# One joint norm between two transformer blocks, squares added up on GpSimd, output stored in pieces, weight splits and first loads in another order

## What is computed

```
h  = rms_norm(x, gain) * (1 + scale) + shift      # ahead of every mixer and every feed-forward net
x  = x + gate * y                                  # after each of them
x1 = rms_norm(x, final_norm_g)                     # end of the first block: the x of the second
h  = rms_norm(x1, norm1_g_2) * (1 + scale) + shift # first thing the second block does
```

## Time and profile before

| | us |
|---|---|
| median of three executions | 3278.46 |
| profiled execution, its own time | 3276.97 |
| span of its trace | 3275.2 |
| TensorE busy | 3024.4 (92%) |
| VectorE busy | 1440.7 (44%) |
| ScalarE busy | 1134.9 (35%) |
| GpSimd busy | 194.5 (6%) |

### The profile page before, as it was taken

One profiled execution on the slowest core, in us unless ns is written; L12 is line 12 of the kernel. 1 busy time (PEld: TensorE's weight loads), 2 busy tenths in 40 slices (PEclk: granted clock), 3 DMA queues, 4 the chain that ended last, 5 costly groups with the idle time before them and its releaser, 6 DMA issues.

```text
span 3275.2 us, 34399 instructions
## 1 busy us (share of the span) xinstructions
PE 3024.4 (92%) x14360; PEld 2379.1 (73%) x14360; DVE 1440.7 (44%) x1884; ACT 1134.9 (35%) x1396; POOL 194.5 (6%) x199
## 2 busy tenths in 40 slices
PE   5998888899999888999998999989899999999998
PEld 3875666678877777857776887777676667778876
DVE  5474444354433554534456434245443344433322
ACT  3364222232222444334543222134433345432221
POOL 0011222000000010001000000000100010000000
PEclk8998787899999999999999999999999999999999
DMA  7430000133433211413223343331131121222221
GB/s 263 174 132 19 1 1 1 60 146 135 155 109 122 79 51 52 171 45 119 71 84 135 142 154 138 119 116 52 46 139 58 67 71 46 96 79 101 91 92 49
DMA packets 46278, 309.68 MB, mean 95 GB/s; under 512 B 5339, under 2 KB 6235, under 8 KB 12844
## 3 DMA queue, kind: packets, MB, share of 16 engines
q1 hardware_dynamic: 43964, 297.32, 25.2%
q0 software_dynamic: 2160, 10.16, 0.9%
HBM read 302.74 MB, written 4.72 MB: 94 GB/s over the span
## 4 chain that ended last, share of the span: by engine, by line
PE 57%; ACT 6%; DVE 3%; issue 2%; POOL 0%; ACTq 0%; DVEq 0%
PE bank L1775 45%; PE bank L1725 3%; PE bank L2015 2%; PE bank L2035 2%; ACT WH L791 1%; PE bank L2156 1%; PE bank L1807 1%; PE bank L2026 1%; PE bank L2151 1%; ACT L853 1%; DVE WL L1243 1%; PE bank L2051 1%; ACT L782 0%; ACT a_KS L1109 0%; PE bank L2020 0%
## 5 line engine op out<-in xcount | busy, mean ns | idle before, releaser
L1775 PE MATMUL bank<-HH,WH 128*128 128x512 f32 x2360 | 957.4, 406 | 49.8 <-DVE HL L1296 34.6
L1775 PE MATMUL bank<-HL,WH 128*128 128x512 f32 x2360 | 929.6, 394 | 0.0
L1775 PE MATMUL bank<-HH,WL 128*128 128x512 f32 x2360 | 929.6, 394 | 0.0
L1243 DVE TENSOR_TENSOR WL<-raw,WH 128x2048 fp32r<-128x2048 f32 (+2 forms) x263 | 483.1, 1837 | 736.1 <-ACT WH L791 735.3
L1775 PEld LDWEIGHTS bank<-HH,WH 128*128 128x128 f32 x2360 | 448.5, 190 | 173.7 <-issue 65.0
L791 ACT ACTIVATE WH<-raw 128x2048 fp32r<-128x2048 f32 (+3 forms) x223 | 395.7, 1775 | 422.8 <-PE bank L1775 416.5
L1775 PEld LDWEIGHTS bank<-HL,WH 128*128 128x128 f32 x2360 | 448.7, 190 | 99.9 <-issue 7.9
L1775 PEld LDWEIGHTS bank<-HH,WL 128*128 128x128 f32 x2360 | 447.2, 189 | 98.7
L1775 PE MATMUL bank<-AH,WH 128*128 128x512 f32 x528 | 213.2, 404 | 8.6 <-DVE AL L1339 8.6
L1775 PE MATMUL bank<-AH,WL 128*128 128x512 f32 x528 | 209.5, 397 | 0.0
L1775 PE MATMUL bank<-AL,WH 128*128 128x512 f32 x528 | 209.4, 397 | 0.0
(11 more groups left out here) (310 smaller groups left out, 3617.5 us busy)
## 6 DMA issues: line engine op xcount, KB each, us to landing
raw<-in_wstream_dram SPq DMA_DIRECT2D x256, 1024.0 KB, 4.9
raw<-in_wstream_dram SPq DMA_DIRECT2D x24, 512.0 KB, 3.4
raw<-in_wstream_dram SPq DMA_DIRECT2D x12, 768.0 KB, 4.2
bgam<-in_consts_dram POOLq DMA_DIRECT2D x2, 1792.0 KB, 7.2
bias_dram<-bias_row POOLq DMA_DIRECT2D x8, 320.0 KB, 2.5
xT<-in_x_dram SPq DMA_DIRECT2D x1, 2048.0 KB
toep<-bias_dram POOLq DMA_DIRECT2D x8, 256.0 KB, 3.0
out_dram<-ost SPq DMA_DIRECT2D x1, 2048.0 KB, 6.3
```

The lines of the kernel that those rows point to most:

```text
L1243: TT(WL[:, wi % 2, now], raw[:, j.load % RAW, now], WH[:, wi % 2, now].bitcast(F32), ALU.subtract).then_inc(s["w_split"], 2 if half is Non ...
L1775: last = MM(o[m][0:cw, :], a, b, start=j.first and u == 0 and q == 0, stop=j.last and u == j.units - 1 and q == 2)
```

## The change

- **Joint norm.** Norms 2 and 3 become one norm (`DOUBLE` = 2). Its sum is that of x·x·(g·g + eps), g being `final_norm_g`: one column `gfin2` = g·g + eps is made at the start, and VectorE, not ScalarE, makes these squares with it (one STT a tile). The scale column is multiplied by g once more. Norms are renumbered, 7 in all.
- **The normed x is made aside.** It is still needed for the later sum x + gate·y. Steps ("renorm", 0 to 4) stand in the first layer of the second block: after job `aqf` and after `abg`, ScalarE squares four tiles each into `esq` and GpSimd adds them up (7 additions); after `av`, TensorE sums once with ones and ScalarE takes Ln and Exp (`er`); behind mixes 0 and 1 of branch A, VectorE scales four tiles each of `xT`. The first `wout` of that layer waits for them.
- **Squares added up on GpSimd.** In norms 1 to 6, GpSimd adds the squares of tiles 0 to 5 (5 additions 128x512 into `nadd`), and TensorE makes one ones-matmul for them, at the norm, beside those of tiles 6 and 7. The two ones-matmuls of each ("square") step are gone.
- **Last output job by row blocks.** The last `wout` and `down` job (`HALVED`) makes all matmuls of its first output tile and then all of its second, with a semaphore `gemm_half` between them, so VectorE can take tile 6 out while tile 7 is made.
- **Splits ahead of the scaling.** For norms 1 to 5 (`EARLY`), the weights of the second job behind the norm are split inside the norm (ScalarE: between the last square and the Ln table; VectorE: ahead of its wait for the Exp), no longer at the first job behind it. At the start, the split of the first job stands right behind the bias copies on ScalarE, and ahead of the seventh ada chunk on VectorE; its load goes ahead of that chunk's.
- **First loads.** `relb` and `onehot` and then x in two halves are issued ahead of the raw loads; 4 constants remain behind them. `bias_row` has eight buffers, so no copy waits for a store. The bias matmuls use banks 6, 7, 2 and 3 and no longer wait for the Exp. The memset and the cast of the masks are moved behind.
- **Stored in four pieces** of 512 KB, each when two tiles are ready.

```diff
         def squares(r, tiles):                      # ScalarE
+            if r == DOUBLE:
+                return
             for k in tiles:
...
-                if k >= 2:
-                    act.wait_ge(s["n_sum"], 8 * r + k - 1)
-                elif ffns(r):
-                    act.wait_ge(s["f_low"], 22 * ffns(r))
+                    if k >= 2:
+                        act.wait_ge(s["n_add"], 5 * (r - 1) + max(k - 2, 1))
+                    elif ffns(r):
+                        act.wait_ge(s["f_low"], 22 * ffns(r))
                 A(nsq[:, k % 2, :], xT[:, k, :], ACT.Square).then_inc(s["n_square"], 1)
         def rstd(r):
             squares(r, LATE[r])
+            if r in EARLY:
+                split(JOBS[EARLY[r]].w + 1)
             ready_ln()
...
+            elif st[0] == "renorm":                 # ScalarE
+                if st[1] < 2:
+                    for k in range(4 * st[1], 4 * st[1] + 4):
+                        A(esq[:, k, :], xT[:, k, :], ACT.Square).then_inc(s["e_square"], 1)
+                elif st[1] == 2:
+                    act.wait_ge(s["e_sum"], 1)
+                    A(er[:, :], bank[6][:, :], ACT.Ln, bias=eps[:, :], scale=1.0 / D).then_inc(s["e_ln"], 1)
+                    act.wait_ge(s["e_ln"], 1)
+                    A(er[:, :], er[:, :], ACT.Exp, scale=-0.5).then_inc(s["e_rstd"], 1)
...
         def ada_chunk(j):                           # VectorE
+            if j.ada == 6:
+                split(0)
...
         def norm(n, r):                             # VectorE
+            if r == DOUBLE:
+                squares(LATE[r])
+            if r in EARLY:
+                split(JOBS[EARLY[r]].w + 1)
             dve.wait_ge(s["n_rstd"], r + 1)
...
+            if st[0] == "square":                   # GpSimd
+                r, c = st[1:]
+                for k in range(2 * c, 2 * c + 2):
+                    if k:
+                        pool.wait_ge(s["n_square"], KD * r + k + 1)
+                        if k == 1:
+                            pool.wait_ge(s["n_rstd"], r)
+                            pool.tensor_tensor(nadd[:, :], nsq[:, 0, :], nsq[:, 1, :], ALU.add
+                                               ).then_inc(s["n_add"], 1)
...
-        def squares(n, r, tiles):                   # TensorE
+        def squares(n, r):
+            if r:
...
+                pe.wait_ge(s["n_add"], 5 * r)
+                MM(bank[4][:, :], ones[:, :], nadd[:, :], start=True, stop=False).then_inc(s["n_sum"], 1)
+            for k in LATE[r]:
+                pe.wait_ge(s["n_square"], KD * r + k + 1)
                 MM(bank[4][:, :], ones[:, :], nsq[:, k % 2, :], start=k == 0, stop=k == KD - 1
                    ).then_inc(s["n_sum"], 1)
```

More of the change, by code:

```diff
@@ L132, in plan @@
     ffn(0)
-    steps.append(("norm", "renorm"))
     for L in range(1, LAYERS2 + 1):
         steps.append(("norm", 2 * L))
-        for kind in ("aqf", "abg", "av"):
+        for x, kind in enumerate(("aqf", "abg", "av")):
             job(kind, L, 0)
+            if L == 1:
+                steps.append(("renorm", x))
         mix("a", L, 0, (("aqf", 1), ("abg", 1)))
+        if L == 1:
+            steps.append(("renorm", 3))
         mix("a", L, 1, (("aqf", 2), ("abg", 2), ("av", 1)))
+        if L == 1:
+            steps.append(("renorm", 4))
         mix("a", L, 2, (("aqf", 3), ("abg", 3), ("ga", 0)))
@@ L263, in jobs_of @@
         if s[0] == "ada":
+            if by_step[n].ada == 6:
+                loads.append(products[0])
             loads.append(by_step[n])
-        elif s == ("norm", 0):
-            loads.append(products[0])
         elif s[0] == "job" and by_step[n].w + 1 < len(products):
@@ L945, in begin @@
             def begin(n):
-                if JOBS[n].w + 1 < len(PRODUCTS):
+                if JOBS[n].w + 1 < len(PRODUCTS) and n not in EARLY.values():
                     split(JOBS[n].w + 1)
@@ L1630, in _ @@
                         end(n)
+                        if st[1:] == ("ka", 0, 3):
+                            dve.wait_ge(s["bias_stored"], 16 * 8)
+                            dve.wait_ge(s["const_in"], 16 * NCONST)
+                            dve.wait_ge(s["ones_set"], 3)
+                            dve.memset(cvb[:, :, :, :], 0.0).then_inc(s["conv_pad"], 1)
                         if st[1] == "av":
                             forget(st[2], 0)
+                elif st[0] == "square" and st[1] == DOUBLE:
+                    squares(range(2 * st[2], 2 * st[2] + 2))
+                elif st[0] == "renorm" and st[1] > 2:
+                    if st[1] == 3:
+                        dve.wait_ge(s["e_rstd"], 1)
+                    for k in range(4 * (st[1] - 3), 4 * (st[1] - 3) + 4):
+                        STT(xT[:, k, :], xT[:, k, :], par("g_final", k), er[:, :], ALU.mult, ALU.mult
+                            ).then_inc(s["renormed"], 1)
                 elif st[0] == "gates":
@@ L1767, in gemm @@
                 cw = min(P, wd)
+                if j.w in HALVED:
+                    for m in range(2):
+                        for u in range(j.units):
+                            wh, wl = (x[:, sl, u * wd + P * m:u * wd + P * m + P] for x in (WH, WL))
+                            xh, xl = (x[:, k0 + u, :] for x in X)
+                            for q, (a, b) in enumerate(((wh, xh), (wh, xl), (wl, xh))):
+                                last = MM(o[m][:, :], a, b, start=j.first and u == 0 and q == 0,
+                                          stop=u == j.units - 1 and q == 2)
+                        last.then_inc(s["gemm_done" if m else "gemm_half"], 1)
+                    return
                 for u in range(j.units * now[0] // PARTS, j.units * (now[-1] + 1) // PARTS):
@@ L2114, in _ @@
                            start=True, stop=True).then_inc(s["c_logit"], 1)
-                elif st[0] == "square":
-                    squares(n, st[1], range(2 * st[2], 2 * st[2] + 2))
+                elif st == ("renorm", 2):
+                    pe.wait_ge(s["e_add"], KD - 1)
+                    MM(bank[6][:, :], ones[:, :], eadd[:, :], start=True, stop=True).then_inc(s["e_sum"], 1)
                 elif st[0] == "job":
```

165 lines of the change are left out of this document (96 added, 69 removed).

## The result

The changed kernel takes 3226.99 us (median of four executions, 3224.95 to 3228.14), the kernel before 3277.8 us beside it. The ratio is 0.9846, 95% interval 0.9831 to 0.986. The span went from 3275.2 to 3224.0 us, at nearly the same mean granted clock (0.959 and 0.957). So 51.2 us of the trace have to be found.

A forecast was written before the change was run, and what follows sets the result against it. The prediction took TensorE's stream of matmuls (57% of the span) as the bound. Its terms, -26.5 + 3.7 - 11.1 + 3.7 - 2.2 - 0.65 - 2.9, gave -36.0 us: forecast 3242 us, range 3232 to 3253.

The forecast's parts named there:

- 15 square steps: Two ones-matmuls a square step leave TensorE's stream between `wout` and `down` output jobs: 15 x 1.77 = -26.5 us.
- splits ahead of the scaling: At norms 1, 4, 6 and 5, the early weight split holds Ln back, less 0.35 us won: +3.7 us, bounds +1.7 to +5.
- joint norm: Between the blocks, one norm for two brings the first matmul to E + 11.4 from 22.5 us: -11.1, or -9.4.
- norm aside: Second block's first layer: Ln and Exp after `av` delay level 1 of mix 0: +3.7 us, bounds 0 to +6.
- start: Bias rows begin earlier, ada chunks 6 and 7 follow the low part; first scaling 58.0 against 60.20: -2.2 us, or -1.1.
- last norm's Ln, store in pieces: At the end, Ln at E + 2.84, not 3.5: -0.65 us; last 512 KB store lands sooner: -2.9, at least -1.5.
- Rival (e): At the norms, ScalarE's table load is not held back by the split, so norms cost nothing extra: 3238 us; chance 0.06.
- rival (a): At the start, TensorE stays at full clock, six bias rows end 5.1 us earlier: 3237 us; chance 0.12.
- Rival (c): Output jobs turn out bound by their splits, so half of the 26.5 us stays: 3255 us; chance 0.06.
- (d): Slower: GpSimd's 37 additions stretch VectorE by 2.2 us each, 81 us if all reaches TensorE: 3323 us; chance 0.01.
- rival (b): GpSimd additions wait for VectorE; sum aside 3 to 5 us after `av`, norms' sums tenths late: 3250 us; chance 0.15.

## Why the prediction was too small

The sum of the forecast against what the traces show, in its own steps:

| step | forecast | shown |
|---|---|---|
| 15 square steps | -26.5 | 1.71 a `down` column, 1.77 a `wout` job: -26.0; taken back, 1.77 each: 26.6 |
| splits ahead of the scaling | +3.7 | norms 0.75 x 3 + 1.06 = +3.3 |
| joint norm | -11.1 | 22.47 to 12.78: -9.7 |
| norm aside | +3.7 | +2.6 at mix 0; +4.6 over the layer of the trace, +5.2 in the time |
| start | -2.2 | 60.20 to 58.17: -2.0 |
| last norm's Ln, store in pieces | -3.55 | E to the end of the span 18.29 to 13.93: -4.4 |
| sum | -36.0 | -34.2 |
| address of A and Y | none | -11.3 to -12.5 |

The two parts make 45.5 to 46.7 of 51.2 us (the norm aside taken at 4.6). The 5 us left have no step of their own. Some 4 of them lie in one stretch, the mixer of the last layer: 705.13 us before and 695.57 after, 9.6 less, where two square steps (3.5) and the address of `Y` (288 x 0.0067 = 1.9) explain 5.4. The kernel with `H` moved by 64, with the same instructions and spacing as before, takes 702.43 us there, so 2.7 us of that stretch differ between executions alone. The whole time of the kernel before ran from 3272.63 to 3279.76 us on one chip. That the rest is of this kind too is likely and not shown: the changed kernel with the address taken back is 38.5 us faster than the kernel before (34 to 44 by its interval), and the steps sum up to 34.2.

**What failed** is the forecast's sum, 3276.97 - 36.0: it adds up what each part of the change removes, adds and moves, and so puts the change in all other instructions at nothing, without a reason. The matmuls of the `down` and `Y` jobs needed a term of 11 to 12 us there (11.3 and 12.5 measured by the two runs with 32 bytes). The forecast read the diff as a list of instructions. The 32 bytes of `gfin2`, for which it has no term, shifted the working memory of every later stage, and 2160 matmuls whose code is untouched came 3% closer together (0.2267 for 0.2333 us). The terms that the sum did have came out at -34.2 for -36.0, and of these the early splits, at +3.3, were a loss as foreseen. The range was built from the bounds of the listed terms (lower ends -47 against the 50.8 measured) and had no room for a term that wasn't on the list. Before the run the trace held half of the clue: in the same kernel the matmuls of `H` start 0.2267 us apart and those of `A` 0.2333 (394 and 397 ns in their means), with nothing to tell them apart but what they read. Why two equal instructions differ is a question that finds this; I did not ask it.

**Point by point.** The `wout` jobs at 10.9 us throughout, `down` columns 1.8 less (1.71, once the address is taken out): right. The `WH` split between square and table, Ln at E + 4.7 (4.64): right, and taking the split away gave E + 2.84 as worked out. Rival (e), the splits pay, is refuted. First matmul of the joint norm at E + 11.4: it came at E + 12.78, since the ones-matmuls of tiles 6 and 7 both ran on the lower clock (four records from 1044.87 to 1048.28 in a row, granted clock 0.56), and the forecast's bound of -9.4 had allowed for one; the gain was 9.7. Level 1 of mix 0 later by 2.5 to 4 us: 2.63. The clock of the start falls at 38 us (granted 1.00 from 36 to 38, 0.59 from 38 to 40, 0.50 behind), first scaling at 58.0 (58.17): right, and rival (a) is out. Rival (c) is out by the 10.88 us of the output jobs, and (d) by the sign. Of rival (b), additions in the way, the stretched instructions are there and the late sum isn't (see below). The four stores land 2.7 us behind their issue and not 3.4: the price was taken from loads of the same size, 3.4 for 2.7, and the term of the end as a whole was 0.8 too small.

**GpSimd's additions.** Their price was the step with the worst size, and at the norms it had no effect. Taken at 1.30 us, they took 5.56 / 2 = 2.8 us beside a low part, which itself took 3.36 for 2.29, and 7.48 / 4 = 1.87 in the norm aside. The row that spoke for it was there: the ada operation of 3.42 us in the earlier trace rows. The Trainium skill, "SBUF — State Buffer", section "Who interferes with whom", has it that a VectorE instruction with two SBUF inputs contends with a GpSimd instruction that reads SBUF, and the low part, which reads `raw` and `WH`, is such an instruction; its 3.36 us agree in kind. The forecast took up to 2.2 us of stretch an addition from the ada row and held the room in the jobs against it, and that was right: nothing waits for GpSimd's sum at any norm. In the norm aside the stretch did reach GpSimd's lane products, by way of VectorE. Without the norm aside `a_QQ` starts 32.37 us behind the layer's first matmul (1087.40 - 1055.03), with it at 36.17, and both times it waits for VectorE's `a_G`. Of the 3.80 us, 2.17 come from ScalarE's four squares ahead of the weight split (the forecast had 2.4), and 1.6 from VectorE's low part (2.94 us for 2.29) and first operation of `forget` (1.78 for 0.81) beside the additions. Level 1 was not held up by it, since it waited last for `a_KS`.

## What to carry to other kernels

Before a change is priced by its instructions, look at what it does to the layout: a new buffer, even of 32 bytes, can move what lies behind it, and an experiment that only adds those bytes to the old kernel separates the two effects. Where two groups of equal instructions have different mean times, find out why; it is a gain or a trap that waits for the next edit. What stands in the chain "last square, Ln, Exp" pays nearly in full (1.73 us a norm for a split of 1.90), so work that is due later than the norm belongs behind it, and the price of a step is better measured by leaving that step out than by comparing two layers of one execution.

## What was new about the hardware

In these kernels a 128x512 matmul follows the one before it after 0.2267 us if the start addresses of its moving operand and of its weights agree modulo 64 bytes (both on a multiple, or both 32 bytes beside one), and after 0.2333 us if they differ by 32; moving both by 64 changes nothing (3277.8 against 3276). A matmul of 128x256 goes the other way: 0.120 us where they agree and 0.117 where they differ. The Trainium skill, "SBUF — State Buffer", section "Who interferes with whom", gives TensorE two read ports for these, independent of each other, and knows contention only between VectorE and GpSimd. The runs show that the time of a matmul depends on how its two SBUF operands lie to each other, which that picture has no place for; by what mechanism, and whether the two reads are what meets, they don't tell. Offsets other than multiples of 32 and two operands 64 apart (modulo 128) were not tried, and other shapes were not looked at.
